# A fused two-layer kernel on one core: the product into the value tile's accumulator goes two places later in each pair, behind the former pair's seventh

## What is computed

```python
def adaln(cvec, w, b):
    m = jax.nn.silu(cvec) @ w + b
    return jnp.split(m, 6, axis=-1)
...
def conv_ffn(h, w_up, conv_w, conv_b, w_down):
    u = dwconv_centered(h @ w_up, conv_w, conv_b)
    g, v = jnp.split(u, 2, axis=-1)
    return (jax.nn.silu(g) * v) @ w_down
```

## Time and profile before

| what | us |
|---|---|
| median of 3 runs | 1927.05 (1926.91 to 1929.3) |
| the profiled execution | 1925.41 |
| its span in the trace | 1923.6 |
| TensorE matmul busy | 1787.4 (93%) |
| VectorE, ScalarE, GpSimd busy | 1045.7, 891.8, 1013.2 |
| mean granted TensorE clock | 0.972 of full speed |
| up projections (L1608), share of the chain that ended last | 12.4% |

### The profile page before, as it was taken

How to read it: one execution, slowest core, us unless ns; L and a number is a source line. 1 busy time by engine, 2 the same in 40 slices (tenths; PEclk the granted TensorE clock), 3 DMA queues, 4 the chain that set the end, 5 groups by cost and what they waited for, 6 DMA issues and landing times. The chain is left out here.

```text
span 1923.6 us, 32461 instructions
## 1 busy us (share of the span) xinstructions
PE 1787.4 (93%) x12581; PEld 1661.4 (86%) x12581; DVE 1045.7 (54%) x1765; ACT 891.8 (46%) x1640; POOL 1013.2 (53%) x743
## 2 busy tenths in 40 slices
PE   6999998799999999989999999989977999999997
PEld 5888787689988998979889898868966999899997
DVE  4555735564256336455666666587155642661553
ACT  4344414455255325433665756574035542652452
POOL 2534353567356636646555555535735663674572
PEclk9999998899999999999999999989978999999999
DMA  9621164243244233433433333243211231322222
GB/s 361 219 94 38 50 236 148 79 143 105 89 149 141 88 107 112 140 121 87 131 115 110 121 91 119 76 121 103 75 49 44 66 99 56 88 78 83 61 82 78
DMA packets 263857, 209.37 MB, mean 109 GB/s; under 512 B 9848, under 2 KB 238237, under 8 KB 263069
## 3 DMA queue, kind: packets, MB, share of 16 engines
q1 hardware_dynamic: 262989, 204.70, 34.6%
q10 hardware_dynamic: 720, 2.62, 0.4%
HBM read 196.63 MB, written 10.67 MB: 108 GB/s over the span
## 5 line engine op out<-in xcount | busy, mean ns | idle before, releaser
L1608 PE MATMUL ps<-comb,w_hi 128*128 128x322 f32 x2464 | 578.9, 320 | 70.0 <-DVE cv L2773 37.1
L1608 PEld LDWEIGHTS ps<-comb,w_hi 128*128 128x128 f32 x2464 | 427.2, 194 | 94.7 <-issue 76.9
L1181 POOL TENSOR_SCALAR w_hi<-raw 128x512 fp32r<-128x512 f32 x158 | 244.5, 1565 | 429.7 <-PE ps L1287 261.3
L1199 POOL TENSOR_TENSOR w_lo<-raw,w_hi 128x512 fp32r<-128x512 f32 (+1 forms) x228 | 285.1, 1254 | 308.1 <-ACT w_hi L2038 307.8
L1608 PE MATMUL ps<-comb,w_lo 128*128 128x322 f32 x1232 | 389.9, 317 | 0.0
L2038 ACT ACTIVATE w_hi<-raw 128x512 fp32r<-128x512 f32 (+1 forms) x228 | 139.1, 614 | 229.2 <-PE ps L1637 183.8
L1608 PEld LDWEIGHTS ps<-comb,w_lo 128*128 128x128 f32 x1232 | 238.4, 193 | 0.0
L1185 POOL TENSOR_TENSOR w_lo<-raw,w_hi 128x512 fp32r<-128x512 f32 x158 | 207.2, 1332 | 0.0
L2695 DVE SCALAR_TENSOR_TENSOR xT<-ps,mod,xT 128x128 f32<-128x128 f32 x112 | 56.6, 547 | 244.4 <-PE ps L1637 199.6
L1287 PE MATMUL ps<-h_hi,w_hi 128*128 128x324 f32 (+1 forms) x640 | 162.2, 335 | 3.3 <-DVE h_lo L2941 3.3
L1637 PE MATMUL ps<-g_hi,w_lo 128*128 128x324 f32 x704 | 161.5, 310 | 0.0
(11 more groups left out here) (376 smaller groups left out, 3491.4 us busy)
## 6 DMA issues: line engine op xcount, KB each, us to landing
raw<-in_ffn_w_up SPq DMA_DIRECT2D x176, 256.0 KB, 3.7
ada<-in_ada_w SPq DMA_DIRECT2D x20, 1024.0 KB, 10.2
ada<-in_ada_w SPq DMA_DIRECT2D x40, 512.0 KB, 4.7
raw<-in_ffn_w_down SPq DMA_DIRECT2D x80, 256.0 KB, 3.3
raw<-in_ssd_w_in SPq DMA_DIRECT2D x40, 512.0 KB, 4.1
R<-scr_acs SPq DMA_DIRECT2D x22, 512.0 KB, 5.2
raw<-in_att_w_in SPq DMA_DIRECT2D x16, 512.0 KB, 6.7
ada_att<-in_ada_w SPq DMA_DIRECT2D x8, 1024.0 KB, 6.9
```

Of the source, the lines that this page charges most:

```text
L1181: nc.gpsimd.tensor_scalar(w_hi[slot][:, a_:b_, :], raw[j][:, a_:b_, :], 1.0, None, ALU.mult).then_inc(w_hi_done, 1)
L1199: nc.gpsimd.tensor_tensor(job_lo_home(j, nk), job_src(job), job_hi_home(j, nk).bitcast(F32), ALU.subtract).then_inc(lo_pool, 1)
L1608: ins = mm(out, w[:, k, :], c[:, k, :], start=x in (1, 2, 3, 5) and (k, n_) == (0, 0), stop=x in (2, 3, 4, 5) and (k, n_) == (3, 2), skip_ ...
```

## The change

In `ffn_schedule` P1(i+1) moves from behind P6(i) to behind P7(i); at the head of a part P2 comes before P1. The duties that hung on P2 in GpSimd's list (`hidden_low`) and on P1 in ScalarE's list (`hidden_high`) now hang on the job that has the same place in the new list, P1 and P2. `up_left` waits for both products, and moves behind `chain_3` and `chain_4` on VectorE. In `ada_half` the two halves swap their waits, as P2's small matmuls now come first; the order of issue stays.

```diff
--- before.py
+++ after.py
@@ -68,9 +68,9 @@
 
     jobs = []
     for p, (m0, n) in enumerate(PARTS):
-        jobs += [("P", 1, m0), ("P", 2, m0), ("P", 5, m0)]
+        jobs += [("P", 2, m0), ("P", 1, m0), ("P", 5, m0)]
         for i in range(m0, m0 + n - 1):
-            jobs += [("P", 6, i), ("P", 1, i + 1), ("P", 2, i + 1), ("P", 7, i), ("P", 3, i), ("P", 5, i + 1),
+            jobs += [("P", 6, i), ("P", 2, i + 1), ("P", 7, i), ("P", 1, i + 1), ("P", 3, i), ("P", 5, i + 1),
                      ("P", 4, i)]
         i = m0 + n - 1
         jobs += [("P", 6, i), ("P", 3, i), ("P", 7, i), ("D", p, 0, 0), ("P", 4, i), ("D", p, 1, 0), ("D", p, 2, 0),
@@ -942,7 +942,7 @@
                 l, j_ = divmod(ADA_J[s // 4], 6)
                 at0 = j_ * D + 4 * P * j
                 src = w_ada[l][:, 2 * (s % 4):2 * (s % 4) + 2, at0:at0 + 4 * P]
-                sp.wait_ge(ada_mm, ada_done(s - 1) - (1 - j if s > 24 else 0))
+                sp.wait_ge(ada_mm, ada_done(s - 1) - (j if s > 24 else 0))
                 sp.dma_start(side_in(j), src).then_inc(ada0_in[4 * j], 16)
 
             def load(slot, t, src, k=KD):
@@ -1245,7 +1245,7 @@
                         last = i == m0 + n_ - 1
                         if job[1] == 6 and i > m0:
                             hidden(l, i - 1)
-                        if job[1] == 2 and i > m0 + 1:
+                        if job[1] == 1 and i > m0 + 1:
                             hidden_low(l, i - 2)
                         if job[1] == 7 and last:
                             hidden_low(l, i - 1)
@@ -2186,7 +2186,7 @@
                             copy_t(l, i + 2)
                         silu(l, i)
                     high_job(j + 4)
-                    if x == 1 and i > m0 + 1:
+                    if x == 2 and i > m0 + 1:
                         hidden_high(l, i - 2)
                     if x == 7 and last:
                         hidden_high(l, i - 1)
@@ -2745,7 +2745,7 @@
             def up_left(l, i):
 
                 dve.wait_ge(p1_copied, FT * l + i + 1)
-                dve.wait_ge(job_mm, job_done(l, ("P", 2, i)))
+                dve.wait_ge(job_mm, max(job_done(l, ("P", x, i)) for x in (1, 2)))
                 if l == 0 and i in ADA_SIDE:
                     side_add(i)
                 tt(py(i), py(i), p1c, ALU.add).then_inc(c11_done, 1)
@@ -2874,9 +2874,9 @@
                     up_sum(l, i)
                     chain_1_low(l, i + 1)
                     chain_2(l, i + 1)
-                    up_left(l, i + 1)
                     chain_3(l, i + 1)
                     chain_4(l, i + 1)
+                    up_left(l, i + 1)
                     low_right(l, i)
                     chain_2_low(l, i + 1)
                     up_right(l, i)
```

## The result

The changed kernel takes **1905.8 us** (median of 4 runs, 1905.14 to 1906.91), the kernel before 1926.98 (4 runs, 1926.73 to 1929.3) beside it. The ratio is 0.989, with a 95% interval of 0.9876 to 0.9905: 21.2 us less, where 18 were forecast. The profiled execution took 1906.16 us.

The account below looks back on a forecast made before the run. TensorE, 93% busy, bounds the kernel; P1's 32 waits of 1.36 us for value taps cost 43.5 us. Layer 1 saves 12.0, layer 0 19.8, less 6.8, 6.4 and 0.6: 18.0 saved, median 1909 us, 8-in-10 range 1901 to 1919.

Parts of the forecast that it names:

- The new name of the wait: Layer 1: P1's 1.36 us wait for value taps becomes P7's 0.57 us wait for `up_sum`, saving 0.79 a pair.
- The ring: Gate-tile path over GpSimd, ScalarE and VectorE: value taps about 0.1 us late behind odd pairs, so 0.75 saved per pair.
- on the clock: Time in us within one pair's period, counted from the end of P4(i-1) on TensorE.
- rival of a longer ring: Ten hand-overs between engines each cost 0.04 us more, 0.4 us a pair: 1917 us; chance 0.19.
- Layer 0: 14 pairs with modulation weights save 1.36 us each, less 0.05; pairs 20 and 21 save 1.5 together: 19.8 us.
- Part heads: P2, now first, waits 1.4 us for the eighth residual at four heads; P6 then waits for `up_left`: 6.8 us lost.
- The late halves: Layer 0: the second half of modulation weights lands 0.6 us late for P2 in 11 pairs: 6.4 us lost, bounds 0 to 15.
- The sum: Whole kernel: 12.0 + 19.8 - 6.8 - 6.4 = 18.6, less 0.6 for first pairs of each layer: 18.0 us saved.
- Halves in time: Rival: layer 0's modulation-weight halves land before P2 needs them, so 24.4 us are saved: 1903 us; chance 0.22.
- renamed wait: Rival: `up_sum` comes 0.9 us later in every pair, P7 waits instead and nothing is left: 1927 us; chance 0.05.
- slower: Rival: two splits ahead of P1's copy on ScalarE delay the taps by 1.1 to 1.2 us: 1936 us; chance 0.04.

Follow-up runs that it names:

- e7_copy_six: Changed kernel with ScalarE's copy of P1 cut into six pieces from a part's third pair on: 1909.48 us, ratio 0.9907.
- e2_halves: Changed kernel with half 1 of layer 0's modulation weights issued before half 0: 1901.78 us, ratio 0.9864.
- e9_after_again: Changed kernel run and profiled again with nothing altered: 1905.6 us, ratio 0.9901.
- e6_sum_back: Changed kernel with P1 third, ahead of P7, and `up_left` back ahead of `chain_3` and `chain_4` on VectorE: 1919.33 us, ratio 0.9957.
- e1_third: Changed kernel with P1(i+1) third, ahead of P7(i), so only one place later than before the change: 1896.5 us, ratio 0.9838.
- e4_sum_first: Changed kernel with `up_sum` ahead of `chain_1` on VectorE, TensorE's order kept: 1899.97 us, ratio 0.9855.

## Why the prediction was right

**The new name of the wait.** "P7 stands still for 0.57 us": measured 0.57, in every pair from a part's third on in layer 1 but one (0.93, in the first part) and in pairs 20 and 21. This was the point that decided between a gain of 1.36 and one of 0.79 a pair, and it came from reading who stands behind the taps on VectorE, not from the wait that was removed.

**The ring.** Forecast for the copy, `up_left` and `up_right` were 8.77, 9.2 and 10.6 on the clock, measured 8.65, 9.11 and 10.52. The value taps were to be 0.1 us late behind odd pairs; they were not late at all. So 0.77 a pair instead of 0.75. e7_copy_six shows that this was close: 0.32 us more in that ring, and the odd pairs lose 0.25. The rival of a longer ring had the right sensitivity for one pair in two and the wrong state: nothing had grown.

**Layer 0.** The period without late halves is 14.02 us (e2_halves), where 14.05 was forecast from 15.39.

**Part heads.** 1.4 us each was forecast, and 1.43 measured; in the timeline of the head at 1607.95 the residual starts at 1606.79 and the weight load pauses until 1607.92:

```profile
1606.79 1.01 DVE L2695 SCALAR_TENSOR_TENSOR xT<-ps,mod,xT 128x128 f32<-128x128 f32 x2
...
1607.92 0.30 PEld L1608 LDWEIGHTS ps<-comb,w_hi 128*128 128x128 f32 x2 [1.43 <-issue]
```

P6 behind it waited 0.51 us in layer 0 (0.5 forecast) and 0.13 in layer 1 (0.1 forecast), as the weight-load row shows it. Undoing the heads gave back 6.9 us; 6.8 was forecast.

**The late halves.** 6.4 us forecast; e2_halves gave back 5.7, and the periods of the kernel after exceed 14.02 by 6.6 in sum, of which 0.6 is left in e2_halves: 6.0. The size was right and the shape wrong, so the sum owes something to luck. I had 0.6 us in each of 11 pairs. In fact eight halves were late, by 0.75 us on average, and a late pair is mostly followed by one on time (in the second part 14.03, 14.76, 14.03, 14.75, 14.02, 15.07), and one half in the first part was late by 2 us. That landing depends on size alone is refuted here: the two halves are equal, and in the kernel after the first of them landed 3.9 to 4.8 us after its issue, the second 4.8 to 6.6. By my count the second was issued in time for any landing under 5.3 us. The Trainium skill (DMA: Bandwidth & Descriptors, Anatomy of one DMA) would have had both halves and the 256 KB ahead of them in within 5.0 us, an estimate from its fit; the trace does not agree (550.28 to 557.42, 7.1 us, for the pair above), and its fit is for transfers that GpSimd issues, where these come from SyncE.

**The sum.** Its terms were 12.0, 19.8, -6.8, -6.4 and -0.6; measured are 12.3, about 20.7 (14 x 1.37 + 2 x 0.77), -6.9 to -7.0, -5.7 to -6.0, and some -0.8: about 19.4 in place of 18.0. The medians differ by 21.2 us (20.9 in e9_after_again, against its own runs of the kernel before). Over two profiles of each kernel the end stretch came out 10.2 us shorter, where I had 9 (12.0 less the heads' 3.0), and the middle 9.4, where the terms as measured add up to 10.8 (20.7 - 3.9 - 6.0) and my forecast ones to 9.6. The rest of the difference between the medians, some 2 us, lies ahead of the first mark (353.8 us before, 351.7 after, on average). It can't be told from scatter, since other kernels with the same opening as the changed one have that mark at 351.8 to 354.0 us. So the forecast of the time is right by its terms to 1.4 us; where the last 2 us come from stays open.

**The rivals.** Halves in time, renamed wait and slower are each contradicted by a row above. For the last, the two splits ahead of the copy did hold it back, by 0.7 us (P1's last matmul ends at 1511.38, the copy starts at 1512.07), but no more than the count had allowed for: `up_left` came 0.1 us earlier than counted, and `up_right` at 10.52 where it was at 11.14 before. That rests on `chain_3` and `chain_4` standing ahead of `up_left`. I wrote that this keeps P6's split off the path, which e6_sum_back bears out, but gave it no price; it is 22.8 us in the kernel with P1 third.

## What to carry to other kernels

When a product waits for a buffer, look for the product that should stand in its place, and work out for each candidate what *it* waits for, on one clock. Moving the waiting product by two places made its neighbour wait; by one place it made none wait, and gave 9.3 us more. Then follow the move into the other lists: the order of transfers (5.7 us here), the first round of a loop, where buffers come free in another order (6.9 us), and the helper on the other engine that would block its queue in its old place.

A ring over several engines whose slack is counted at zero is no loss in itself. Here it starts afresh in each period with a read that waits for a product (the value tile's, 0.27 us behind P4), and that start moves along when the period gets shorter. What counts is the way from there to the taps that TensorE asks for: one split less on it, 0.45 us, and P2 no longer had to wait at a period of 12.47 us (e1_third against e4_sum_first). A trial that lengthens one of its steps by a few tenths tells in one run how much slack there is (e7_copy_six). And a wait's name is worth a check against the ends of all that the product waits for: in e6_sum_back a row named a low part that was another product's.

## What the runs showed of the hardware

- Two 512 KB transfers that SyncE issued half a microsecond apart, most of them behind one of 256 KB and with another 0.5 us behind them, landed 3.9 to 4.8 us (the first) and 4.8 to 6.6 us (the second) after their issue, over the 20 times in the kernel after. The order of issue alone moved 5.7 us of the middle stretch and 4.0 us of the median, with no byte more or less.
- A ScalarE copy of 128x322 took 0.43 us, and the same copy in six pieces of 54 columns 0.75 us in all, although each piece is recorded with 0.22 to 0.28 us: back-to-back pieces overlap. I had estimated 0.3 to 0.9 us more; it was 0.32. The Trainium skill (ScalarE: Activation LUTs, What ACT_TABLE_LOAD costs) gives 186 ns plus 0.833 ns per column for such an instruction, by which 54 columns would take 231 ns, an estimate, and the trace agrees (0.24 us); with its overlap of 93 ns between neighbours six pieces would take 0.92 us, an estimate, where the run shows 0.75.
- A waiting helper can cost more than a waiting product: in e6_sum_back 2.3 us of idle time on VectorE, on an engine busy for 54% of the span, became 1.1 to 1.5 us on TensorE in each pair.
